# Out projection opened as four side-by-side units without its last two row blocks; norm sums, third gates and first-pass pieces moved later

## Chip, cores, metric

One NeuronCore of one Trainium2 chip runs the whole kernel in one launch. The metric is device time in microseconds (us) of that core, median over runs.

## What is computed

One layer of a hybrid decoder over 2048 prompt tokens with 16 meta tokens ahead of them, and over 8 running sequences of 4 tokens (2096 columns in all, 1024 model dimensions, fp32). A normalised input goes through one input projection. One half of its output feeds an RG-LRU group (causal convolution over 4 taps, two gates, a linear scan), the other half an HGRN2 group (4 heads of 128, gated linear attention with a matrix state). Both outputs, joined, go through one output projection; a squared-ReLU MLP follows.

```python
u = (hn @ w_in)                                  # xa, ga, qb, fb, ib, gb
xc = conv_b + sum(xpad[:, j:j+T] * cw[j] for j in range(4))
r, ig = sigmoid(xh @ w_ra + b_ra), sigmoid(xh @ w_rx + b_rx)
y_a = scan(a, bt) * gelu(ga)
o = rms(hgrn2(silu(q), k, v, logf)) * gn * silu(g)
x = x + concat([y_a, o]) @ w_out
x = x + square(relu(rmsnorm(x) @ w_up)) @ w_down
y = rmsnorm(x)
```

## The kernel before

The columns are worked in two passes (`p` = 0 and 1): 1024 columns in two tiles of 512, then 1072 in three tiles of 358, 358 and 356. Each weight matrix is cut into blocks of 128 output rows, 96 blocks in all: 20 for the four head iterations (V, gate G, XA, F, Q of each), 4 for the GELU gates (GA), 8 for the output projection, 64 for the MLP. A **unit** is one block by one tile: 8 row blocks (the 128-deep slices of the contraction), each with three matmuls, since every fp32 value is split in a rounded high part and a low rest (`hi*hi`, `hi*lo`, `lo*hi`, L411 to L413). A **half unit** is 4 row blocks, 12 matmuls. Units rotate through 4 PSUM banks (`bank`), everything else through 4 more (`aux`). A unit opens when the unit four before it has been read out of its bank.

`schedule(p)` is a table written out by hand: after which half unit (a **slot**, numbered from 0 within an iteration) a **piece** of the attention or gate work is issued. Iteration `i` computes the projections of head `i` and, between them, the pieces of head `i-1`; iteration 4 has the four GA blocks and head 3's pieces. The pieces: VT (transpose v), D (diagonal scores), L1 to L7 (the levels of the decay products, each needing what DVE made of the one before), KT, U (state updates), O (outputs), SS (sum of squares), S1, S2 (reciprocals) and S3 (norm and gate products, DVE alone). GATE is the RG-LRU gates' matmuls, RS, N2 and NF are the ones-matmuls of the three norms, FN and FY the final norm of pass 0, done inside pass 1. `SLOTS` gives the slots, `GATE_SLOT` that of GATE, `FINAL_SLOTS` those of NF, FN and FY.

All engines walk the same table. PE issues (L393 on), DVE reads units out of the banks and does the level products, the state recurrence (`s_in`, eight steps, L1028, semaphore `s_step`; O waits for step `s7`), the convolution (`convolve`, right behind the read-out of the last XA tile, L1137 to L1145), the gate chain and the scan (L1058 to L1076), the reciprocals (L1048) and S3 (L1052, L1054). ACT does sigmoids, square roots, copies and the rounding of activations (`a_hi`), all at the helper's line L601. DVE and ACT run strictly in the order written. In pass 0 the weights come by DMA (SP), ACT rounds them (`round_weights`), DVE or, from the output projection on, POOL makes the low part (L368); in pass 1 POOL's queue reloads the kept parts (L380, L381).

Behind the table, ACT rounds the mixed activations `xy` into `a_hi`, DVE subtracts to `a_lo` (L1233), and PE runs the 8 blocks of the output projection in the order `OUT_ORDER` of row blocks, of which the last, 3, is head 3's. `xy` is then reloaded with the residual by ACT's queue. DVE adds each unit to it (L1243), ACT writes `b_hi` and a square, DVE writes `b_lo` (L1245) and adds up the squares (L1251). The sums over partitions (N2) go to PE once all squares are added; then the MLP starts.

## Time and profile before

| | us |
|---|---|
| median of three runs | 2595.76 |
| the three runs | 2594.53 to 2601.26 |
| profiled execution, its own time | 2603.55 |
| span of that execution, first to last instruction | 2601.9 |
| PE busy in the span | 2493.0 (96%) |
| DVE busy | 1038.5 (40%) |
| ACT busy | 593.5 (23%) |
| POOL busy | 284.1 (11%) |
| granted TensorE clock, mean share of full speed | 0.982 |

The profiled execution took 7.8 more than the median, and its time is 1.65 more than its span. All moments named below are in us from the start of the span. In a row of the timeline the bracket gives the idle time of that engine just before the instruction and what ended it; "x16" is the number of instructions merged in the row. One fp32 matmul of the kernel's `aux` pieces shows as two instructions.

### The profile page before, as it was taken

How to read it: one execution, taken by the hardware profiler on the slowest of the kernel's cores; microseconds unless marked ns; L12 is line 12 of the kernel's file. 1: busy time of each engine (PE TensorE's matmuls, PEld its weight loads, DVE VectorE, ACT ScalarE, POOL GpSimd, SP SyncE). 2: the span in 40 equal slices, each digit the busy share in tenths (PEclk: the TensorE clock that was granted, in tenths of full speed). 3: DMA queues.
4: the chain of work that ended last, by engine and by line, in shares of the span. 5: the costliest groups of instructions: out<-in, count | busy, mean ns of one | idle time of the engine just before them, and what ended most of it. 6: DMA issues, size and time to landing. Idle time of an engine off the chain costs nothing.

```text
span 2601.9 us, 33392 instructions
## 1 busy us (share of the span) xinstructions
PE 2493.0 (96%) x13358; PEld 2235.6 (86%) x13358; DVE 1038.5 (40%) x1603; ACT 593.5 (23%) x961; POOL 284.1 (11%) x275
## 2 busy tenths in 40 slices
PE   5999998999999999999899999999999999999996
PEld 4778877878888888888898988989999999999995
DVE  6676776332121121123756576654321211211224
ACT  4233233332031121223223032132210200200211
POOL 0000001212222122222000000000000000000000
PEclk9999999999999999999999999999999999999998
DMA  5222224434434444353412122133222232222223
GB/s 192 97 98 80 91 97 144 140 133 146 137 141 145 145 139 147 126 204 144 151 61 69 50 65 65 50 142 98 81 81 97 81 97 82 95 85 92 89 89 104
DMA packets 86620, 284.32 MB, mean 109 GB/s; under 512 B 14096, under 2 KB 17296, under 8 KB 86544
## 3 DMA queue, kind: packets, MB, share of 16 engines
q1 hardware_dynamic: 41472, 151.01, 16.9%
q0 software_dynamic: 27648, 100.68, 11.8%
q10 hardware_dynamic: 17424, 31.57, 3.4%
q8 instruction: 53, 0.87, 0.1%
q14 instruction: 23, 0.19, 0.0%
HBM read 171.54 MB, written 111.68 MB: 109 GB/s over the span
## 4 chain that ended last, share of the span: by engine, by line
PE 88%; DVE 9%; ACT 1%; issue 1%; ACTq 1%; DVEq 0%
PE bank L411 26%; PE bank L413 26%; PE bank L412 26%; PE aux L470 4%; DVE ea L1048 1%; DVE attn L979 1%; PE aux L536 1%; PE aux L424 1%; PE aux L460 1%; DVE k L951 1%; DVE a_lo L1187 1%; PE aux L494 1%; DVE q L950 1%; PE aux L513 1%; PE aux L512 1%
## 5 line engine op out<-in xcount | busy, mean ns | idle before, releaser
L411 PE MATMUL bank<-a_hi,w_hi 128*128 128x358 f32 (+2 forms) x2560 | 929.7, 363 | 45.1 <-DVE a_lo L1187 20.6
L413 PE MATMUL bank<-a_hi,w_lo 128*128 128x358 f32 (+2 forms) x2560 | 911.6, 356 | 0.0
L412 PE MATMUL bank<-a_lo,w_hi 128*128 128x358 f32 (+2 forms) x2560 | 910.9, 356 | 0.0
L411 PEld LDWEIGHTS bank<-a_hi,w_hi 128*128 128x128 f32 x2560 | 488.6, 191 | 96.5 <-issue 35.1
L412 PEld LDWEIGHTS bank<-a_lo,w_hi 128*128 128x128 f32 x2560 | 489.2, 191 | 46.9 <-issue 2.9
L413 PEld LDWEIGHTS bank<-a_hi,w_lo 128*128 128x128 f32 x2560 | 488.6, 191 | 45.8
L411 PE MATMUL bank<-b_hi,w_hi 128*128 128x512 f32 (+2 forms) x1280 | 452.9, 354 | 0.0
L413 PE MATMUL bank<-b_hi,w_lo 128*128 128x512 f32 (+2 forms) x1280 | 452.4, 353 | 0.0
L412 PE MATMUL bank<-b_lo,w_hi 128*128 128x512 f32 (+2 forms) x1280 | 452.1, 353 | 0.0
L1274 DVE TENSOR_TENSOR xy<-xy,bank 128x356 f32 (+3 forms) x160 | 94.6, 591 | 564.5 <-PE bank L413 564.5
L368 POOL TENSOR_TENSOR w_lo<-w_st,w_hi 128x1024 fp32r<-128x1024 f32 x74 | 180.9, 2445 | 1045.8 <-ACT w_hi L601 1045.8
L601 ACT ACTIVATE a_hi<-tmp 128x356 f32 (+3 forms) x160 | 88.7, 555 | 833.7 <-DVE tmp L1263 833.7
L411 PEld LDWEIGHTS bank<-b_hi,w_hi 128*128 128x128 f32 x1280 | 240.8, 188 | 23.8 <-issue 0.8
L412 PEld LDWEIGHTS bank<-b_lo,w_hi 128*128 128x128 f32 x1280 | 240.9, 188 | 23.7 <-issue 0.5
L413 PEld LDWEIGHTS bank<-b_hi,w_lo 128*128 128x128 f32 x1280 | 240.6, 188 | 22.0
L1263 DVE SCALAR_TENSOR_TENSOR tmp<-bank,rs 128x356 f32<-128x356 f32 (+1 forms) x160 | 95.1, 594 | 350.4 <-PE bank L413 349.4
L380 POOL DMA_DIRECT2D w_hi<-kept_hi x96 | 50.8, 530 | 1218.9 <-PE bank L413 1218.9
L1266 DVE TENSOR_TENSOR a_lo<-tmp,a_hi 128x356 f32 (+3 forms) x160 | 95.3, 595 | 197.4 <-ACT tmp L601 197.4
L601 ACT ACTIVATE w_hi<-w_st 128x1024 fp32r<-128x1024 f32 x96 | 100.8, 1051 | 277.4 <-PE bank L413 271.9
L470 PEld LDWEIGHTS aux<-q,k 128*128 128x128 f32 x896 | 106.5, 192 | 20.7 <-DVE f L953 18.9
L470 PE MATMUL aux<-q,k 128*128 128x64 f32 x896 | 108.9, 274 | 10.6 <-DVE f L953 10.1
L979 DVE COPY_PREDICATED attn<-mask,aux 128x512 f32<-128x512 int32 (+2 forms) x72 | 50.8, 739 | 96.5 <-PE aux L470 96.5
(150 smaller groups left out, 1557.3 us busy)
## 6 DMA issues: line engine op xcount, KB each, us to landing
w_st<-in_wall SPq DMA_DIRECT2D x96, 512.0 KB, 4.1
kept_hi<-w_hi SPq DMA_DIRECT2D x96, 512.0 KB, 4.8
kept_lo<-w_lo SPq DMA_DIRECT2D x96, 512.0 KB, 5.6
w_hi<-kept_hi POOLq DMA_DIRECT2D x96, 512.0 KB, 3.9
w_lo<-kept_lo POOLq DMA_DIRECT2D x96, 512.0 KB, 4.7
xs<-in_xT ACTq DMA_DIRECT2D x8, 536.0 KB, 6.9
xy<-in_xT ACTq DMA_DIRECT2D x8, 536.0 KB, 6.9
xs<-in_xT ACTq DMA_DIRECT2D x16, 256.0 KB, 6.3
```

What stands on the lines that cost most here:

```text
L368: pool.tensor_tensor(w_lo[:, slot, :], w_st[:, slot, :], w_hi[:, slot, :].bitcast(F32), ALU.subtract).then_inc(w_ready, 1)
L380: pool.dma_start(w_hi[:, slot, :], kept_hi[m]).then_inc(w_again[slot], 16)
L411: pe.matmul(ps, wh, xh, start=(j == 0), stop=False)
L412: pe.matmul(ps, wh, xl, start=False, stop=False)
L413: mm = pe.matmul(ps, wl, xh, start=False, stop=(j == 7))
L424: pe.matmul(open_bank(a)[:, 0:n], ones[:, :], src[:, c0:c0 + n], start=True, stop=True).then_inc(aux_done, 1)
L470: mm = pe.matmul(ps[:, 64 * c:64 * c + 64], k[:, CH * c:CH * c + CH], qv[:, c, :, 1, :], start=True, stop=True)
L601: return nc.scalar.activation(out, in_, func, **kw)
L979: dve.copy_predicated(dst, mk.broadcast_to([r_, nc_, w // x, x]), src).then_inc(aux_free[u % 4], 1)
L1263: stt(z, bank[lu % 4][:, 0:w], 0.0, rs[:, c0:c0 + w], ALU.max, ALU.mult).then_inc(bank_free[lu % 4], 1)
L1266: tt(a_lo[:, 4 * qd + j, c0:c0 + w], z, a_hi[:, 4 * qd + j, c0:c0 + w].bitcast(F32), ALU.subtract).then_inc(h_ready, 1)
L1274: tt(x, x, bank[lu % 4][:, 0:w], ALU.add).then_inc(bank_free[lu % 4], 1)
```

## The change

- `SLOTS[0]`: in pass 0 VT stays at slot 0 and every piece behind it moves one slot later; `GATE_SLOT[0]` goes from 16 to 17. In iteration 4, S1, S2 and S3 leave the table and stand behind it.
- `GATE2`: in pass 1 the gates of the third tile are issued one half unit after the first two (only PE has this piece).
- `FINAL_SLOTS`: NF, FN and FY of pass 0 move from slots 3, 4, 5, 8 to 15 of pass 1 to 8, 9, 10, 12 to 19.
- Output projection: the first four units run row blocks 0, 1, 2, 4, 5, 6 (`EARLY` = 6) one after another, then the last two (7 and 3) of each; the rest run in natural order. ACT and DVE prepare the six blocks of all tiles but the last one during the last GA unit, then the last tile's six, then (DVE) the reciprocals and products of head 3, then the last two blocks of all tiles.
- N2: the first MLP unit is issued ahead of the wait for the squares and the norm sums, with a wait on each `b_lo` tile. For this the first two groups of the MLP's loop are written out.

```diff
+SPLIT_UNITS = 4
+EARLY = 6
...
+def y_no(p, t, n):
+
+    base = KB * NT[0] * p
+    return base + (EARLY * t + n if n < EARLY else EARLY * NT[p] + (KB - EARLY) * t + n - EARLY) + 1
...
-SLOTS = [dict(zip(range(16), PIECES)),
+SLOTS = [dict(zip([0] + list(range(2, 17)), PIECES)),
          dict(zip([0, 4, 5, 6, 8, 9, 10, 12, 13, 14, 15, 16, 18, 19, 21, 22], PIECES))]
-GATE_SLOT = [16, 24]
+GATE_SLOT = [17, 24]
...
-FINAL_SLOTS = {3: ("NF", 0), 4: ("FN", 0), 5: ("FN", 1), **{8 + b: ("FY", b) for b in range(8)}}
+FINAL_SLOTS = {8: ("NF", 0), 9: ("FN", 0), 10: ("FN", 1), **{12 + b: ("FY", b) for b in range(8)}}
...
-                    if i >= 1 and s in SLOTS[p]:
+                    if i >= 1 and s in SLOTS[p] and not (i == HEADS and SLOTS[p][s] in ("S1", "S2", "S3")):
                         pieces.append((SLOTS[p][s], i - 1))
                     if i < HEADS and s == GATE_SLOT[p]:
                         pieces.append(("GATE", i))
+                    if p and i < HEADS and s == GATE_SLOT[p] + 1:
+                        pieces.append(("GATE2", i))
...
+                    for t in ([2] if name == "GATE2" else [0, 1]):
+                        c0, w = TILES[p][t]
...
+                units = [(m, t) for m in range(KB) for t in range(nt)]
+                for m, t in units[:SPLIT_UNITS]:
+                    if t == 0:
+                        weights(p, OUT0 + m)
+                    open_unit(unit_no(p, OUT0 + m, t))
+                    out_unit(m, t, list(range(EARLY)))
+                for m, t in units[:SPLIT_UNITS]:
+                    out_unit(m, t, list(range(EARLY, KB)))
+                for m, t in units[SPLIT_UNITS:]:
+                    if t == 0:
+                        weights(p, OUT0 + m)
+                    open_unit(unit_no(p, OUT0 + m, t))
+                    out_unit(m, t, natural)
...
+                            if first and lu == 0:
+                                pe.wait_ge(b_sum, (KB - 1) * sum(NT[:p + 1]))
+                                for t2, (c2, w2) in enumerate(TILES[p]):
+                                    ones_sum(AUX[(p, "N2", 0)] + t2, rs, c2, w2)
...
+                    if half and blk == OUT0 - 1 and t == NT[p] - 1:
+                        for t2 in range(NT[p] - 1):
+                            round_mix(t2, range(EARLY))
...
+                if p == 0:
+                    round_weights(OUT0 + 1)
+                round_mix(NT[p] - 1, range(EARLY))
...
+                reload_x(range(EARLY))
+                for t in range(NT[p]):
+                    round_mix(t, range(EARLY, KB))
+                reload_x(range(EARLY, KB))
...
+                mix_rest(nt - 1, range(EARLY))
+                for name in ("S1", "S2", "S3"):
+                    piece(p, name, HEADS - 1)
+                for t in range(nt):
+                    mix_rest(t, range(EARLY, KB))
```

Three places in the order of instructions matter below. The first is DVE in iteration 1 of pass 0, around the read-out of the second XA tile (`xpad<-bank`), the convolution (`xc`) and the state recurrence (`s_in`, `state`). Before:

```order
L1105 TENSOR_TENSOR xpad<-bank,rs 128x512
L1118 TENSOR_TENSOR gate<-gate,tmp 128x512
L1016 COPY s_in<-state 128x128
L1028 SCALAR_TENSOR_TENSOR s_in<-s_in,f,aux 128x128 x7
L1028 SCALAR_TENSOR_TENSOR state<-s_in,f,aux 128x128
L1105 TENSOR_TENSOR xpad<-bank,rs 128x512
L1137 COPY xpad<-xhist 128x3
L1143 TENSOR_SCALAR xc<-xpad,par 128x1024
L1145 SCALAR_TENSOR_TENSOR xc<-xpad,par,xc 128x1024 x3
```

After (the same lines of code have other numbers):

```order
L1154 TENSOR_TENSOR xpad<-bank,rs 128x512
L1186 COPY xpad<-xhist 128x3
L1192 TENSOR_SCALAR xc<-xpad,par 128x1024
L1194 SCALAR_TENSOR_TENSOR xc<-xpad,par,xc 128x1024 x3
L1065 COPY s_in<-state 128x128
L1077 SCALAR_TENSOR_TENSOR s_in<-s_in,f,aux 128x128 x7
L1077 SCALAR_TENSOR_TENSOR state<-s_in,f,aux 128x128
```

Before, U stands in slot 10, and its recurrence comes ahead of the second XA tile; after, U stands in slot 11, whose half unit completes that tile, so the read-out and the whole convolution come first.

The second is ACT in the same iteration, from the last F sigmoids to the gates' sigmoids (`ta`, `k_tok`); `tmp<-q` is the sigmoid of the first Q tile. Before:

```order
L601 ACTIVATE k<-f 128x512
L601 ACTIVATE f<-f 128x512
L601 ACTIVATE w_hi<-w_st 128x1024
L601 ACTIVATE ta<-aux,par 128x512
L601 ACTIVATE k_tok<-aux,par 128x512
L601 ACTIVATE ta<-aux,par 128x512
L601 ACTIVATE k_tok<-aux,par 128x512
L601 ACT_TABLE_LOAD
```

After:

```order
L638 ACTIVATE k<-f 128x512
L638 ACTIVATE f<-f 128x512
L638 ACTIVATE w_hi<-w_st 128x1024
L638 ACTIVATE tmp<-q 128x512
L638 ACTIVATE ta<-aux,par 128x512
L638 ACTIVATE k_tok<-aux,par 128x512
L638 ACTIVATE ta<-aux,par 128x512
L638 ACTIVATE k_tok<-aux,par 128x512
L638 ACT_TABLE_LOAD
```

The sigmoid of the first Q tile, which needs DVE to have read that tile out, now stands ahead of the gates' sigmoids. DVE in turn reads that tile behind S3 (`xy<-xy,par,ea`, `xy<-xy,gate`) and ahead of the gate chain:

```order
L1097 RECIPROCAL ea<-ea 128x512
L1263 TENSOR_TENSOR w_lo<-w_st,w_hi 128x1024
L1101 SCALAR_TENSOR_TENSOR xy<-xy,par,ea 128x1024
L1103 TENSOR_TENSOR xy<-xy,gate 128x1024
L1154 TENSOR_TENSOR q<-bank,rs 128x512
L1174 TENSOR_SCALAR f<-f,lbv 128x512
L1175 TENSOR_SCALAR k<-k,lbv 128x512
L1177 TENSOR_SCALAR f<-f 128x512
```

The third is ACT behind the table in pass 0, from the last GELU to the third weight rounding. Before:

```order
L601 ACTIVATE xc<-xc 128x512 x2
L601 ACTIVATE w_hi<-w_st 128x1024
L601 ACTIVATE a_hi<-xy 128x512 x16
L623 DMA xy<-in_xT 128x1024 x8
L601 ACTIVATE b_hi<-xy,par 128x512
L601 ACTIVATE rs<-xy 128x512
L601 ACTIVATE b_hi<-xy,par 128x512
L601 ACTIVATE rs<-xy 128x512
L601 ACTIVATE w_hi<-w_st 128x1024
```

After:

```order
L638 ACTIVATE xc<-xc 128x512
L638 ACTIVATE w_hi<-w_st 128x1024
L638 ACTIVATE a_hi<-xy 128x512 x6
L660 DMA xy<-in_xT 128x1024 x6
L638 ACTIVATE a_hi<-xy 128x512 x4
L660 DMA xy<-in_xT 128x1024 x2
L638 ACTIVATE b_hi<-xy,par 128x512
L638 ACTIVATE rs<-xy 128x512
L638 ACTIVATE b_hi<-xy,par 128x512
L638 ACTIVATE rs<-xy 128x512
L638 ACTIVATE w_hi<-w_st 128x1024
```

The rounding of the mixed activations is now in three parts, and the third weight rounding (block 26) still follows two read-outs of output units.

## Rows read from the trace of the kernel before

**Rows 1.** The page, part 1: busy time, share of the span, instructions
```profile
PE 2493.0 (96%) x13358; PEld 2235.6 (86%) x13358; DVE 1038.5 (40%) x1603; ACT 593.5 (23%) x961; POOL 284.1 (11%) x275
```

**Rows 2.** Stretches: us, then PE, PEld, DVE, ACT, POOL busy (instructions), clock, DMA
```profile
432.90:438.50 5.60, 5.60 (x13) 4.42 (x14) 5.60 (x10) 4.07 (x8) 0.00 (x0) 0.50 0.67 252
585.00:650.00 65.00, 65.00 (x282) 52.66 (x281) 13.12 (x19) 14.00 (x20) 14.40 (x6) 1.00 0.43 146
1885.00:1950.00 65.00, 65.00 (x399) 65.00 (x399) 13.23 (x25) 7.27 (x17) 5.27 (x10) 1.00 0.24 81
```

**Rows 3.** Waits of PE: who for whom, us in total, times, longest us
```profile
PE bank L411 <- DVE a_lo L1233: 15.8, 2, 9.5
PE aux L460 <- DVE q L1120: 8.1, 4, 2.0
PE aux L536 <- ACT ta L601: 6.4, 3, 2.2
PE aux L424 <- DVE rs L1251: 6.1, 2, 3.4
PE aux L424 <- ACT rs L601: 5.6, 1, 5.6
```

**Rows 4.** Timeline of PE in the first pass: start us, us, instruction, idle before
```profile
99.96 2.95 PE L460 MATMUL aux<-q,k 128*128 128x128 f32 x16 [2.03 <-DVE q L1120]
...
187.37 2.02 PE L460 MATMUL aux<-q,k 128*128 128x128 f32 x16 [2.01 <-DVE q L1120]
...
229.10 1.95 PE L494 MATMUL aux<-v_tok,k_tok 128*128 128x128 f32 x16
...
233.66 0.38 PE L512 MATMUL aux<-q,s_in 128*128 128x128 f32 x2
...
240.00 1.88 PE L424 MATMUL aux<-q,ones 128*128 128x512 f32 x4
```

**Rows 5.** Timeline of DVE, the same iteration: state steps, convolution
```profile
230.19 3.07 DVE L1028 SCALAR_TENSOR_TENSOR s_in<-s_in,f,aux 128x128 f32<-128x128 f32 x7 [3.13 <-PE aux L494]
...
233.86 0.69 DVE L1105 TENSOR_TENSOR xpad<-bank,rs 128x512 f32<-128x512 f32 x1 [0.15 <-PE bank L413]
...
235.70 3.92 DVE L1145 SCALAR_TENSOR_TENSOR xc<-xpad,par,xc 128x1024 f32<-128x1024 f32 x3
```

**Rows 6.** Timelines of DVE (two stretches) and ACT around the gates
```profile
183.41 0.69 DVE L1105 TENSOR_TENSOR q<-bank,rs 128x512 f32<-128x512 f32 x1
...
185.20 0.68 DVE L1105 TENSOR_TENSOR q<-bank,rs 128x512 f32<-128x512 f32 x1
...
245.29 6.56 DVE L1048 RECIPROCAL ea<-ea 128x512 f32<-128x512 f32 x2
...
254.80 1.23 DVE L1054 TENSOR_TENSOR xy<-xy,gate 128x1024 f32<-128x1024 f32 x1
255.94 1.22 DVE L1206 TENSOR_TENSOR w_lo<-w_st,w_hi 128x1024 fp32r<-128x1024 f32 x1
...
254.43 0.67 ACT L601 ACTIVATE ta<-aux,par 128x512 f32<-128x512 f32 x1
```

**Rows 7.** Timelines of PE, DVE and POOL at the first out projection
```profile
432.89 0.77 PE L411 MATMUL bank<-a_hi,w_hi 128*128 128x512 f32 x1 [9.49 <-DVE a_lo L1233]
...
428.88 3.26 DVE L1054 TENSOR_TENSOR xy<-xy,gate 128x1024 f32<-128x1024 f32 x1
...
427.95 3.11 POOL L368 TENSOR_TENSOR w_lo<-w_st,w_hi 128x1024 fp32r<-128x1024 f32 x1 [11.87 <-ACT w_hi L601]
...
449.94 2.40 POOL L368 TENSOR_TENSOR w_lo<-w_st,w_hi 128x1024 fp32r<-128x1024 f32 x1 [18.88 <-ACT w_hi L601]
```

**Rows 8.** Timeline of PE at the norm sums of the first pass
```profile
528.00 3.42 PE L424 MATMUL aux<-rs,ones 128*128 128x512 f32 x4 [3.44 <-DVE rs L1251]
```

**Rows 9.** Timeline of DVE at the start of the second pass
```profile
1270.24 0.97 DVE L1105 TENSOR_TENSOR v<-bank,rs 128x358 f32<-128x358 f32 x2
```

**Rows 10.** Timeline of DVE after the second iteration's gates, second pass
```profile
1427.63 0.53 DVE L1105 TENSOR_TENSOR q<-bank,rs 128x358 f32<-128x358 f32 x1
```

More of the change, by code:

```diff
@@ L154, in aux_uses @@
 def aux_uses(p, name):
-    if name in ("FN", "FY", "S1", "S2", "S3"):
+    if name in ("FN", "FY", "S1", "S2", "S3", "GATE2"):
         return 0
@@ L400, in weights, with products @@
                     pe.wait_ge(w_ready, blk + 1)
-            def half_unit(u, slot, hi, lo, c0, n, korder, half, ready=None, first=0):
+            def products(u, slot, hi, lo, c0, n, korder, js, ready=None, count=None):
                 ps = bank[u % 4][:, 0:n]
-                for j in range(4 * half, 4 * half + 4):
+                for j in js:
                     if ready is not None:
-                        pe.wait_ge(ready, first + j)
+                        pe.wait_ge(ready, count(j))
                     kb = korder[j]
@@ L413, in half_unit, with halves @@
                     mm = pe.matmul(ps, wl, xh, start=False, stop=(j == 7))
-                if half:
+                if js[-1] == KB - 1:
                     mm.then_inc(unit_done, 1)
+            def halves(half):
+                return list(range(4 * half, 4 * half + 4))
             def open_bank(a):
@@ L530, in piece @@
                         ones_sum(a + s, q, lo_, hi_ - lo_)
-                elif name == "GATE":
-                    pe.wait_ge(rg_step, rg_at(p, i, "sc3" if p else "c3"))
-                    for t, (c0, w) in enumerate(TILES[p]):
+                elif name in ("GATE", "GATE2"):
+                    if name == "GATE":
+                        pe.wait_ge(rg_step, rg_at(p, i, "sc3" if p else "c3"))
+                    a = AUX[(p, "GATE", i)]
+                    for t in ([2] if name == "GATE2" else [0, 1]):
+                        c0, w = TILES[p][t]
                         for g, wt in enumerate((w_ra, w_rx)):
@@ L569, in _, with out_unit @@
-                pe.wait_ge(b_sum, (KB - 1) * sum(NT[:p + 1]))
-                for t, (c0, w) in enumerate(TILES[p]):
-                    ones_sum(AUX[(p, "N2", 0)] + t, rs, c0, w)
-                pe.wait_ge(b_lo_ready, KB * (nt + (NT[0] if p else 0)))
-                hb = p * 8 * NT[0] * FF_GROUPS
-                with pe.Fori(0, FF_GROUPS) as g:
+                def out_unit(m, t, js):
+                    products(unit_no(p, OUT0 + m, t), (OUT0 + m) % 2, a_hi, a_lo, *TILES[p][t], OUT_ORDER, js,
+                             y_ready if m == 0 else None, lambda j: y_no(p, t, j))
@@ new lines, in _, with quad @@
+                hb = p * 8 * NT[0] * FF_GROUPS
+                def quad(g, stage, qd, first=False):
+                    for j in range(4):
+                        blk = MLP0 + 8 * stage + j
+                        if p:
+                            pe.wait_ge(w_again[j % 2], 256 * g + 64 * qd + 32 * (blk // 2 + 1))
+                        else:
+                            pe.wait_ge(w_ready, 16 * g + 4 * qd + (blk + 1))
+                        for t, (c0, w) in enumerate(TILES[p]):
+                            lu = j * nt + t
+                            pe.wait_ge(bank_free[lu % 4], 4 * nt * g + nt * qd
+                                       + (unit_no(p, MLP0 + 8 * stage, 0) // 4 + lu // 4))
+                            if stage and j == 0:
+                                pe.wait_ge(h_ready, 8 * nt * g + (hb + 7 * nt + t + 1))
+                            hi, lo = (a_hi, a_lo) if stage else (b_hi, b_lo)
+                            for half in range(2):
+                                products(lu, j % 2, hi, lo, c0, w, natural, halves(half),
+                                         b_lo_ready if first and j == 0 else None,
+                                         lambda kb: KB * NT[0] * p + kb * nt + t + 1)
+                            if first and lu == 0:
+                                pe.wait_ge(b_sum, (KB - 1) * sum(NT[:p + 1]))
+                                for t2, (c2, w2) in enumerate(TILES[p]):
+                                    ones_sum(AUX[(p, "N2", 0)] + t2, rs, c2, w2)
@@ L576, in _ @@
+                quad(0, 0, 0, first=True)
+                quad(0, 0, 1)
+                with pe.Fori(0, 2) as qd:
+                    quad(0, 1, qd)
+                with pe.Fori(1, FF_GROUPS) as g:
                     for stage in range(2):
                         with pe.Fori(0, 2) as qd:
[L578 to L594 removed]
@@ L790, in _, with round_mix @@
                     load_state(0)
+                def round_mix(t, ns):
+                    c0, w = TILES[p][t]
+                    act.wait_ge(unit_done, unit_no(p, OUT0 - 1, t) + 1)
+                    for n in ns:
+                        b = OUT_ORDER[n]
+                        if b < HEADS:
+                            act.wait_ge(o_inv, O_STEPS * (4 * p + b) + O_STEPS)
+                        else:
+                            act.wait_ge(post, post_no(p, 3, b - HEADS, NT[p] - 1) + 1)
+                        fn(a_hi[:, b, c0:c0 + w], xy[:, b, c0:c0 + w], ACT.Copy).then_inc(y_hi, 1)
                 queue = []
@@ L1211, in _ @@
                         started = True
+                    if half and blk == OUT0 - 1 and t == nt - 1:
+                        for t2 in range(nt - 1):
+                            mix_rest(t2, range(EARLY))
                     if half:
```

62 lines of the change are left out of this document (16 added, 46 removed).

## The prediction

> **What bounds the kernel now.** The page's busy times come first: PE is busy for 2493.0 of the span's 2601.9 [rows 1], so no other engine is the bound, and what can be won is the time in which PE stands or runs slowly. The stretches give PE's pace: 282 matmuls of 512 columns in 65 us (0.231 each) and 399 of 358 or 356 columns (0.163 each) [rows 2]. So a half unit, 12 matmuls, takes 2.77 in the first pass and 1.96 in the second. The first of those stretches also shows the other level of the clock: behind a long stand PE starts only 13 matmuls in 5.6 us at a granted clock of 0.50, which is 1.2 GHz; at full clock it would have started 24, so some 2.6 are lost. The waits of PE then name where it stands [rows 3]: twice for the mixed activations ahead of the out projection (15.8), four times for the query at piece D (8.1), three times for an aux bank at the gates' third tile (6.4), twice for the squares ahead of the norm sums (6.1), once for ACT's square root at the start of the second pass (5.6). That is 42.0, and the change is aimed at all of it. The question is what is late next at each place.
>
> **First pass, piece O.** U now follows slot 11, which completes the second XA tile, and DVE works strictly in its written order: tile read-out, convolution, and only then the state recurrence. Before, O followed U's start by 233.66 - 229.10 = 4.56 [rows 4] without a wait. Read-out and convolution take from 233.86 to 235.70 + 3.92 = 239.62, that is 5.76, beginning 0.2 behind the half unit; the seven state steps that O waits for take from 230.19 on, 3.07 [rows 5]. With 0.2 for the copy of the state and 0.2 for the signal, O can start 0.2 + 5.76 + 0.2 + 3.07 + 0.2 = 9.4 after U's start, so PE waits 9.4 - 4.56 = 4.9. Iterations 1 to 3 have a convolution: **+14.7**. Iteration 4 has two GELU operations of about 0.65 in its place: **+0.4**.
>
> **First pass, piece D.** D and GATE both move by one slot, and from the sums SS to D there are as many half units and pieces as before, so PE reaches D just as long after SS. What changes is the query. Before, ACT's first gate sigmoid came at 254.43, 14.4 after the sums at 240.00 [rows 4, 6]. Now the first Q tile's sigmoid stands ahead of it, and DVE reads that tile only behind both reciprocals (6.56), S3 and the weight split, which ended at 255.94 + 1.22 = 257.16, 17.2 after the sums [rows 6]. The first reciprocal can start about 0.9 sooner, with the F read-out behind it, giving 16.3; with 0.7 for the read-out and 0.6 for its sigmoid the gates' sigmoids start at 17.6, 3.2 later than before. In return the chain behind the scan is shorter by the first Q read-out and F's finishing, 185.20 - 183.41 = 1.8 [rows 6]. The wait of 2.0 becomes 2.0 + 3.2 - 1.8 = 3.4 in iterations 2 to 4. Iteration 1 follows an iteration with no head behind it, DVE is free for the tile, and the wait falls to 2.0 - 1.8 = 0.2. In all 10.4 where 8.1 stood: **+2.4**. The short waits between the levels L1 to L3 stay, as both their sides keep their distance.
>
> **The clock in the first pass.** The trace does not show gaps of 3.4 and 4.9 here. Nearest are: a gap of 2.03 with D's sixteen matmuls taking 2.95, and one of 2.01 with 2.02 for the same work [rows 4], so that a gap may cost nothing; and the 2.6 lost behind a gap of 9.49 [rows 2, 7]. I take 2.2 behind each of three waits of 4.9 and 1.2 behind each of three of 3.4, together 10.2, less the 3.5 that the present D gaps cost in the first and last iteration (0.9 in D and about as much behind it): **+6.7**, with 0 - 3.5 and 6 x 2.6 - 3.5 = 12.1 as the ends. By the Trainium skill, TensorE: Matmul & The Clock Gate, section HAM oscillation, stands of this kind send the clock to its lower level each time; by it the term would be its upper end.
>
> **First out projection.** Counted from the end of the last GA half unit, PE before stood 9.49, ran four units of 24 matmuls (22.1) and lost 2.6 [rows 2, 7]: 34.2 to block 26. After, four units with six row blocks give 16.6 of work. DVE ends the six last-tile subtractions at 7.7, the reciprocals 6.6 later and the products 2.5 later, at 16.8, and the last four subtractions at 19.3; PE ends the four units at 23.1, nearly without a stand. But block 26 may be rounded only when block 24's units are done, and its rounding stands on ACT behind two read-outs of output units. Before they were early, and POOL's split behind it, at 449.94, took 2.40 [rows 7]. Now they come in a burst: DVE reads at 19.3 and, after ACT's two operations and `b_lo`, at 22.6; ACT rounds at 24.6 to 25.7, POOL splits until 28.2. PE stands from 23.1 to 28.3 and loses 2 at low clock behind it. The rounding of block 25 adds a split beside DVE's subtractions. Before, a split and DVE's product of two SBUF operands ran side by side, 3.11 and 3.26, where alone they take 2.40 and 1.23 [rows 6, 7]: I add 2.0. GPSIMD Engine Reference, Specifications, in the Trainium skill has the two engines share their SBUF interfaces when DVE has two SBUF inputs; by this rule, the trace agrees. Were there no sharing, the term would be 2.0 better. 28.3 + 2 + 2 = 32.3: **-1.9** (0 to -6, where no clock is lost and no split disturbs).
>
> **Norm sums.** The first MLP unit (5.5, and 3.9 in the second pass) covers the waits of 3.4 and 2.7 [rows 3, 8]; the four sums took 3.42 where four of the same size take 1.88 at full clock [rows 4, 8]. Two waits, 6.1, twice 1.5 and about 0.2 behind each: **-9.5**. What is late next is DVE's reciprocal of the norm (6.6), with three more free banks, 16.6 of PE work, to cover it.
>
> **Start of the second pass.** NF no longer waits 5.6 for ACT. But unit 4 opens in the bank of the first V tile, which DVE reads only at 1270.24, behind the reciprocals of RS [rows 9]. PE came to NF's wait, which ended at 1262.4, at 1256.8, one sum behind slot 3, so without NF it ends slots 4 to 7 7.8 after 1255.7, at 1263.5, and stands until 1270.8; with 2.4 of low clock and 1.7 for NF behind slot 8 it is at 1274.9, where it now is at about 1262.4 + 1.1 + 7.8 + 2.5 = 1273.8: **+1.1** (ends -2 and +3).
>
> **Third gates.** The half unit hides the 2.1 [rows 3]. But the second V tile (slot 2 of the next iteration) opens in the bank of the first Q tile, which DVE reads behind the gate chain, at 1427.63 to 1428.1 [rows 10]; PE reached it at about 1428.7 (an estimate: a gate wait that ended at 1411.2, two sums, seven half units of 1.96, VT and 2 of low clock). So only some 0.6 of slack, and 0.6 more where ACT's last sigmoid comes sooner, is kept: -2.5 over three iterations. In iteration 0 ACT waited for nothing, the chain shifts by the half unit: +1.9. The stand moved to slot 2 costs clock that slack had hidden, 1 each: **+3** (-4 to +7).
>
> **Second out projection.** PE's four early units last 11.8, while DVE needs about 17.7 for subtractions, reciprocals and products; the last two row blocks start 6 later. The wait of 15.8 - 9.5 = 6.3 [rows 3] comes back inside: **-0.7** (-3 to +2).
>
> Sum: 14.7 + 0.4 + 2.4 + 6.7 - 1.9 - 9.5 + 1.1 + 3 - 0.7 = +16.2. The profiled execution's own 2603.55 becomes 2619.8. It stood 7.8 above the median of 2595.76; the median becomes **2612.0**.
>
> **Rivals.**
> Faster: piece O does not wait. What decides is whether DVE is through with convolution and seven steps within 4.56 of U's start; by the rows it needs 9.4, so it would have to run in another order than written. For it: before, it was in time. Then 14.7 and its 6.6 of clock fall away: 2595.8 - 5.1 = 2590.7. Chance 0.12.
> Same: all waits come, but with no clock lost behind them (as at 187.37) and no split beside the subtractions. 10.2 in the first pass, 2 + 2 at the out projection and 1 at the gates fall away: 16.2 - 15.2 = +1.0, 2596.8; with half of it 2604. Chance 0.16.
> Slower still: each new stand pays the whole 2.6: 12.1 for 6.7, and 3 more in the second pass: 2620.4. The 9.49 gap speaks for it, 187.37 against it. Chance 0.12. That is what the section of the Trainium skill's TensorE page named above would give.
> The change does not do what it says in the second pass, where six row blocks are too little work: that is within the forecast.
>
> **How the numbers follow.** The forecast has 0.60. A measurement of this kernel can tell about 0.3%, 7.8, from no change. Slower than 2603.6: nearly all of the forecast, the costlier clock and a little of the second rival, 0.72; within 2588.0 to 2603.6: 0.16; faster: 0.12. The range runs from 2597 (the second rival) to 2624 (the clock at its upper end, with the gates' end).
>
> **What would show it.** Right: in the waits of PE, O (the matmul on `s_in`) for DVE's state steps, three times near 4.9, and D for the query near 0.2 once and 3.4 three times; the wait for N2 and the 9.5 gone; a wait of about 5 for the split of block 26; near 7 for a V read-out at the start of the second pass; about 6 inside its out projection. PEclk lower in the first pass. Wrong: no wait at O, or D waits gone in all iterations.

## The result and the profile after

| | before | after |
|---|---|---|
| median, us (five runs each, interleaved) | 2595.76 | 2611.21 |
| lowest to highest | 2594.53 to 2601.69 | 2609.63 to 2615.19 |
| profiled execution, its own time | 2603.55 | 2615.19 |
| its span | 2601.9 | 2613.5 |
| granted clock, mean | 0.982 | 0.980 |

The ratio is 1.0054, with a 95% interval from 1.0042 to 1.0065: the change makes the kernel slower by 15.45. Forecast were 2612.0, a range of 2597 to 2624, and 0.72 for slower. The two profiled executions differ by less, 11.6, as the one before stood 7.8 above its median and the one after 4.0; so what is read from their rows is good to a few us.

A stand is time in which PE has nothing that it may start. The waits of PE in the kernel after the change (who for whom, us in total, times, longest us), to be read against [rows 3]:

```profile
PE bank L423 <- DVE a_lo L1236: 21.1, 3, 17.2
PE aux L528 <- DVE s_in L1077: 14.4, 4, 4.7
PE bank L423 <- DVE v L1154: 14.2, 2, 8.7
...
PE aux L476 <- DVE q L1169: 8.7, 4, 2.8
PE bank L423 <- DVE q L1154: 7.8, 4, 2.0
PE bank L423 <- DVE a_lo L1252: 7.7, 2, 5.5
PE bank L423 <- POOL w_lo L380: 4.0, 1, 4.0
```

What the change was aimed at is gone: no wait for the squares `rs`, none for ACT's square root, no aux bank held by `ta`, and the wait ahead of the out projection has fallen from 15.8 to 7.7. In its place stand four groups that were not there: piece O for the state (14.4), a bank held by a Q tile (7.8), 5.6 more for a V tile (14.2 where 8.7 stood), and POOL's weight split (4.0). D's wait for the query stayed. The first row is the wait at the kernel's start, which the change does not touch.

Where O and D stand, in the timeline of PE of the same kernel (start us, us, instruction, idle before), first pass:

```profile
154.63 0.79 PE L528 MATMUL aux<-q,s_in 128*128 128x128 f32 x2 [4.73 <-DVE s_in L1077]
...
197.03 3.75 PE L476 MATMUL aux<-q,k 128*128 128x128 f32 x16 [2.81 <-DVE q L1169]
...
251.08 0.80 PE L528 MATMUL aux<-q,s_in 128*128 128x128 f32 x2 [4.72 <-DVE s_in L1077]
...
293.06 2.02 PE L476 MATMUL aux<-q,k 128*128 128x128 f32 x16 [2.81 <-DVE q L1169]
...
387.37 3.63 PE L476 MATMUL aux<-q,k 128*128 128x128 f32 x16 [2.81 <-DVE q L1169]
```

And DVE ahead of the O at 251.08:

```profile
241.82 0.69 DVE L1154 TENSOR_TENSOR xpad<-bank,rs 128x512 f32<-128x512 f32 x1 [4.32 <-PE bank L425]
...
243.68 3.93 DVE L1194 SCALAR_TENSOR_TENSOR xc<-xpad,par,xc 128x1024 f32<-128x1024 f32 x3
247.64 0.23 DVE L1065 COPY s_in<-state 128x128 f32<-128x128 f32 x1
247.97 3.05 DVE L1077 SCALAR_TENSOR_TENSOR s_in<-s_in,f,aux 128x128 f32<-128x128 f32 x7
```

DVE is idle for 4.32 until the XA tile is complete, then works without a pause: read-out, convolution, copy, seven state steps. U had started at 241.62, so O comes 9.46 behind it; the forecast had 9.4.

To see the clock, the stretches from one D to the next (us, PE busy (instructions), granted clock, DMA share, GB/s). They hold the same work. Before:

```profile
99.96:187.37 87.41, 84.52 (x444) 0.98 0.26 91
187.37:273.17 85.80, 82.89 (x445) 1.00 0.27 92
```

After:

```profile
103.45:197.03 93.58, 85.15 (x445) 0.96 0.25 85
197.03:293.06 96.03, 87.60 (x444) 0.95 0.24 83
293.06:387.37 94.31, 85.90 (x445) 0.96 0.25 84
```

PE's *busy* time grew too, by 0.6 in the first of these stretches and 4.7 in the second, for the same instructions, where the mean clock fell to 0.95 and 0.96. That part of the loss stands in no list of waits.

The first out projection, in the timelines of PE, DVE, POOL and ACT of the kernel after (the last GA half unit ends at 449.4):

```profile
455.95 0.77 PE L423 MATMUL bank<-a_hi,w_hi 128*128 128x512 f32 x1 [2.23 <-DVE a_lo L1252]
...
479.72 0.80 PE L423 MATMUL bank<-a_hi,w_hi 128*128 128x512 f32 x1 [4.03 <-POOL w_lo L380]
...
446.88 3.71 DVE L1252 TENSOR_TENSOR a_lo<-xy,a_hi 128x512 fp32r<-128x512 f32 x6 [3.20 <-ACT a_hi L638]
...
453.36 2.44 DVE L1252 TENSOR_TENSOR a_lo<-xy,a_hi 128x512 fp32r<-128x512 f32 x1 [0.77 <-ACT a_hi L638]
...
452.88 2.37 POOL L380 TENSOR_TENSOR w_lo<-w_st,w_hi 128x1024 fp32r<-128x1024 f32 x1 [17.12 <-ACT w_hi L638]
...
477.32 2.34 POOL L380 TENSOR_TENSOR w_lo<-w_st,w_hi 128x1024 fp32r<-128x1024 f32 x1 [22.07 <-ACT w_hi L638]
...
475.68 0.61 ACT L638 ACTIVATE rs<-xy 128x512 f32<-128x512 f32 x1
476.20 1.04 ACT L638 ACTIVATE w_hi<-w_st 128x1024 fp32r<-128x1024 f32 x1
```

The first early unit ends at 453.6 and the second, which reads the last tile, stands 2.23: the first subtraction of that tile, begun while POOL's split ran, took 2.44, where six alone took 3.71. The last two row blocks come without any wait. Block 26's weights are late by 4.03, as its rounding (476.20) stands on ACT behind two read-outs.

In the second pass, timelines of PE and DVE of the kernel after:

```profile
1289.15 0.67 PE L423 MATMUL bank<-a_hi,w_hi 128*128 128x358 f32 x1 [5.56 <-DVE v L1154]
...
1345.97 0.43 PE L423 MATMUL bank<-a_hi,w_hi 128*128 128x358 f32 x1 [1.86 <-DVE q L1154]
...
1745.64 0.67 PE L423 MATMUL bank<-a_hi,w_hi 128*128 128x358 f32 x1 [5.45 <-DVE a_lo L1252]
...
1281.66 6.88 DVE L970 RECIPROCAL rs<-rs 128x358 f32<-128x358 f32 x3 [4.70 <-DMA spad<-in_conv]
1288.57 1.40 DVE L1154 TENSOR_TENSOR v<-bank,rs 128x358 f32<-128x358 f32 x3
```

The norm sums behind the first MLP unit, in PE's timeline, now come without a stand and at full clock:

```profile
553.49 1.88 PE L440 MATMUL aux<-rs,ones 128*128 128x512 f32 x4
```

The two waits removed at the start of the second pass and at its gates are each followed by one on the next thing that was late: the V tile that DVE reads only behind its reciprocals (5.56 where ACT's square root cost 5.6), and a Q tile's bank (1.86 to 2.04, four times) where the gates had waited 2.1 three times.

### The profile page after: what moved, and what is told of

Read it like the earlier page. It is cut to its first block, busy times and chain, and to the rows that moved or that the text cites. A ratio compares the mean times of both kernels' runs of the same rounds, so it can differ in the third digit from the quotient of the medians.

```text
span 2613.5 us, 33374 instructions
## 1 busy us (share of the span) xinstructions
PE 2497.5 (96%) x13358; PEld 2241.2 (86%) x13358; DVE 1039.8 (40%) x1603; ACT 596.2 (23%) x963; POOL 283.4 (11%) x275
## 3 DMA queue, kind: packets, MB, share of 16 engines
q0 software_dynamic: 27648, 100.68, 11.8%
## 4 chain that ended last, share of the span: by engine, by line
PE 73%; DVE 8%; issue 3%; ACT 1%; POOL 0%; DMA 0%; ACTq 0%; DVEq 0%; POOLq 0%
PE bank L423 23%; PE bank L425 23%; PE bank L424 22%; PE aux L486 2%; DVE ea L1097 1%; DVE attn L1028 1%; DVE k L1000 1%; DVE xc L1194 1%; DVE q L999 1%; DVE xy L1123 0%; DVE a_lo L1236 0%; DVE xy L980 0%; PE aux L476 0%; ACT ta L638 0%; PE aux L510 0%
## 5 line engine op out<-in xcount | busy, mean ns | idle before, releaser
L638 ACT ACTIVATE tmp<-tmp 128x356 f32<-128x356 f32 (+1 forms) x160 | 86.1, 538 | 0.0
```

What stands on the lines that cost most here:

```text
L638: return nc.scalar.activation(out, in_, func, **kw)
```

## The experiments

Each variant has 4 to 11 timed executions, beside 15 or 21 of the kernel before. The median of the latter was 2596.03, 2596.04 and 2596.38 in the three groups of four (runs 1 to 4; 5 to 8; 9 to 12), so that times of different groups can be compared. The first group asks whether the first pass's pieces carry the loss, and which wait carries which part.

**1. Pieces back.**

```diff
-SLOTS = [dict(zip([0] + list(range(2, 17)), PIECES)),
+SLOTS = [dict(zip(range(16), PIECES)),
-GATE_SLOT = [17, 24]
+GATE_SLOT = [16, 24]
```

> The changed kernel with the first-pass pieces back in slots 0 to 15 and the first gates in slot 16; the split out projection, the late norm sums and the third gates stay. Theory (the moved pieces cost the first pass some 24 us): the four O waits of 4.7, 4.7, 4.7 and 0.2 go, the four D waits come back at 2.0 each (8.1 in all, as before the change) in place of 8.7, and the clock loss behind the O and D waits (some 7 to 9 us over the pass) goes; the first pass ends 22 to 25 us earlier, and the kernel takes 2586 to 2590 us, 6 to 9 below the kernel before. Rival (the out projection's split and the norm sums, not the pieces, are what costs): the time stays above 2600 us.

Measured: 2585.62 (2582.34 to 2587.37), ratio to before 0.9961, interval 0.9947 to 0.9975. That is 25.6 below the changed kernel, 0.4 beyond the better end of the expected range. O does not wait, D waits four times, 8.1 in all. The theory holds: the table of slots costs 25.6, and all the rest of the change together gains 10.4 over the kernel before.

**2. Convolution behind the pieces (first pass).**

```diff
                         if un[1] == 5 * un[0] + XA and un[0] < HEADS and un[2] == nt - 1:
-                            convolve(p, un[0])
+                            if p:
+                                convolve(p, un[0])
+                            else:
+                                conv_due = un[0]
...
                     for name, i in pieces:
                         if name not in ("RS", "NF", "GATE2"):
                             piece(p, name, i)
+                    if conv_due is not None:
+                        convolve(p, conv_due)
+                        conv_due = None
```

> The changed kernel, with VectorE's convolution of the first pass issued behind the pieces of its slot instead of ahead of them, so that the recurrence U, its read-outs and s_in come first. Theory (O waits because the convolution stands ahead of U on VectorE): the O waits of 4.7 go, the D waits stay at 2.8, 14.4 us of waiting and up to 3 us of clock loss come back, some 2594 to 2598 us. Rival (the s_in chain is bound by something else, or the convolution, now later, makes the D or q step later by as much): less than 5 us come back, over 2606 us.

Measured: 2590.55 (2585.11 to 2594.9), ratio 0.9978 (0.9969 to 0.9988): 20.7 below the changed kernel, more than expected. DVE and PE in the timeline of this variant:

```profile
233.23 0.69 DVE L1154 TENSOR_TENSOR xpad<-bank,rs 128x512 f32<-128x512 f32 x1 [4.33 <-PE bank L425]
233.83 0.22 DVE L1065 COPY s_in<-state 128x128 f32<-128x128 f32 x1
234.16 3.06 DVE L1077 SCALAR_TENSOR_TENSOR s_in<-s_in,f,aux 128x128 f32<-128x128 f32 x7
...
238.64 3.92 DVE L1194 SCALAR_TENSOR_TENSOR xc<-xpad,par,xc 128x1024 f32<-128x1024 f32 x3
...
237.59 0.38 PE L528 MATMUL aux<-q,s_in 128*128 128x128 f32 x2
```

The same operations, with the state steps ahead of the convolution; O starts 4.56 behind U's 233.03, as before the change [rows 4], and without a stand. D still waits 2.8. So the O wait is VectorE's order and nothing else. Of the 20.7, the vanished waits are 14.2; the other 6.5 I put down to the clock (the executions of this variant lie up to 9.8 apart, so this share is rough). The forecast had priced the clock behind the three O waits at 2.2 each, 6.6; my expectation for this run, up to 3, was the poorer number.

**3. The first gates in slot 16, the pieces still moved.**

```diff
-GATE_SLOT = [17, 24]
+GATE_SLOT = [16, 24]
```

> The changed kernel with only the first pass's gates back in slot 16, the pieces still moved. Theory (D of the next head waits for q because the gates' steps on the other engines come one slot later): the D waits of 2.8 go or fall under 0.5, the O waits stay at 4.7; 8 us of waiting and up to 3 us of clock loss come back, some 2599 to 2604 us. Rival (D's wait hangs on the pieces alone): D still waits 2.0 or more, and the time stays at 2609 to 2612 us.

Measured: 2596.56 (2594.41 to 2601.17), ratio 1.0006 (0.9997 to 1.0015), 14.65 below the changed kernel: beyond the expected range on the good side. The wait for `q` has left the list of waits altogether, O's four waits stand at 14.4. Waits of 8.7 and some 6 of clock came back. So D hangs on how far the gates stand ahead of it, not on where D is.

**4. Both edits.**

> Both edits: the convolution behind the pieces of its slot and the first gates in slot 16, with the pieces still one slot later than before. Theory (the two waits are independent): neither O nor D waits over 0.5 us, some 23 to 27 us come back, 2584 to 2588 us, the fastest of the four. Rival (one wait is what holds the other back): the sum of the two gains is not reached, and this is at 2590 us or above.

Measured: 2578.03 (2571.96 to 2579.61), ratio 0.9926 (0.9913 to 0.994): 33.2 below the changed kernel and 18 below the kernel before. Expected had been 23 to 27; again clock is what was priced too low. The gains of runs 2 and 3 add up to 35.4, within what the medians scatter; the two waits are independent. The stretches from D to D of this variant, with the columns as above:

```profile
102.23:185.82 83.59, 82.70 (x445) 1.00 0.28 95
185.82:269.45 83.63, 82.72 (x446) 1.00 0.29 95
```

This is what an iteration takes without a stand: 83.6, at full clock. It is the yardstick for the others. The changed kernel's 93.58, 96.03 and 94.31 hold 7.5 of waits each (4.7 and 2.8), so 2.5, 4.9 and 3.2 are clock; the kernel before has 2.0 of waits in each, and 1.8, 0.2 and 0.2 of clock.

**5. The slots alone, on the kernel before.** The same two lines of run 1 the other way round, and S1 to S3 of the last head behind the table:

```diff
-                    if i >= 1 and s in SLOTS[p]:
+                    if i >= 1 and s in SLOTS[p] and not (i == HEADS and SLOTS[p][s] in ("S1", "S2", "S3")):
...
+                for name in ("S1", "S2", "S3"):
+                    piece(p, name, HEADS - 1)
```

> The kernel before the change, with one part of the change alone: the first-pass pieces one slot later, the first gates in slot 17, and the last head's weight split S1 to S3 behind the table. Theory (the moved pieces cost the first pass what the changed kernel lost there): O waits 4.7 three times, D 2.8 three times, with their clock loss, about 24 us, and the wait ahead of the out projection grows by a half unit, 2.8, as the last head's sums SS come so much nearer to its end: 2619 to 2625 us. Rival (the loss comes only together with the split out projection or the late norm sums): under 2612 us.

Measured: 2627.99 (2627.52 to 2628.49), ratio 1.0116 (1.01 to 1.0131), 32 above the kernel before and 3 beyond the expected range. The waits of this variant:

```profile
PE bank L411 <- DVE a_lo L1236: 23.8, 2, 12.0
...
PE aux L512 <- DVE s_in L1028: 14.4, 4, 4.7
...
PE aux L460 <- DVE q L1120: 8.7, 4, 2.8
```

O and D wait exactly as in the changed kernel, with none of its other parts there. What I had missed is the second pass: S1 to S3 leave its table too, so DVE comes to its reciprocals later, and the wait ahead of the out projection grows in both passes, by 2.5 and by 5.5 (12.0 and 11.8 where 9.5 and 6.3 stood [rows 3]). The 24 that were expected for O, D and their clock, and these 8.0, give the 32; with the 25.6 of run 1 they would give 33.6, so the split into parts is good to a us or two. The full change, with its split out projection, has waits of 2.2 and 5.5 in these two places.

**6. Block 26's weights rounded earlier, on top of run 4.**

```diff
-                    if m and p == 0:
+                    if m > 1 and p == 0:
                         round_weights(OUT0 + m + 1)
                     for t, (c0, w) in enumerate(TILES[p]):
...
+                        if p == 0 and m == 0 and t == 1:
+                            round_weights(OUT0 + 2)
```

> The variant with the convolution behind the pieces and the first gates in slot 16, and in addition the first pass rounds block 26's weights ahead of the second output unit's read-out on ScalarE. Theory (the wait of 4.0 for POOL's split of block 26 is ScalarE's order, read-outs ahead of the rounding): the wait falls to 1 to 2, with less clock loss behind it; 2.5 to 5 us come back, some 2573 to 2576 us. Rival (the rounding cannot start earlier, since it also needs block 24's units done, or the read-outs that it passes free banks that are needed): no gain, 2577 us or more.

Measured: 2573.38 (2570.94 to 2573.96), ratio 0.9906 (0.9891 to 0.9921), 4.65 below run 4, as expected; but the intervals of the two ratios touch (run 4 has 0.9913 to 0.994), so the times alone leave the size open. ACT, POOL and PE of this variant:

```profile
435.85 0.61 ACT L638 ACTIVATE rs<-xy 128x512 f32<-128x512 f32 x1
436.37 1.04 ACT L638 ACTIVATE w_hi<-w_st 128x1024 fp32r<-128x1024 f32 x1
437.88 0.72 ACT L638 ACTIVATE b_hi<-xy,par 128x512 fp32r<-128x512 f32 x1 [0.47 <-DVE xy L1312]
...
437.50 2.37 POOL L380 TENSOR_TENSOR w_lo<-w_st,w_hi 128x1024 fp32r<-128x1024 f32 x1 [19.50 <-ACT w_hi L638]
...
439.92 0.50 PE L423 MATMUL bank<-a_hi,w_hi 128*128 128x512 f32 x1 [1.41 <-POOL w_lo L380]
```

The rounding now stands between the first and the second read-out (the two `b_hi`), and the wait is 1.41 where it was 4.04. Behind the wait of run 4 the granted clock stood at 0.50 for 3.4 us; behind this one it stayed at 1.00.

**7. Third gates back beside the first two, on top of run 4.**

```diff
-                    if p and i < HEADS and s == GATE_SLOT[p] + 1:
-                        pieces.append(("GATE2", i))
...
-                    for t in ([2] if name == "GATE2" else [0, 1]):
+                    for t in range(NT[p]):
```

> The variant with the convolution behind the pieces and the first gates in slot 16, with the second pass's third gates back beside the first two. Theory (the third gates' move gained about 1.3: the aux waits of 2.1 went, the slot 2 bank waits of 1.9 to 2.0 came, but clock that stood low before the change did not drop): the ta wait comes back three times at 2.1, the slot 2 waits go, 0 to 2.5 us slower than that variant, 2578 to 2581 us. Rival (my forecast: the move costs 3): 2 to 4 us faster, 2574 to 2576 us.

Measured: 2575.63 (2574.04 to 2576.47), ratio 0.9912 (0.9896 to 0.9927), 2.4 below run 4. The wait for `ta` is back, 5.8 over three times, and the bank wait for a Q tile (7.9 in run 4) is gone from the list. The forecast's sign is the better one, my later reading of the two profiles (a gain of 1.3) was not; but the intervals of runs 4 and 7 overlap, and in run 9 against run 6 the same edit brings only 0.7. It gains nothing to move these gates; that it costs 3 isn't settled.

**8. PE's order in the out projections plain again, on top of run 4.**

```diff
-SPLIT_UNITS = 4
+SPLIT_UNITS = 1
```

> The variant with the convolution behind the pieces and the first gates in slot 16, with TensorE's order in the out projections as plain units again (each unit all eight row blocks; VectorE and ScalarE keep the order six, then two). Theory (the split covers the wait for the last two row blocks): the first unit stands 11 to 12 in the first pass and some 14 in the second, the wait for block 26's split goes; 8 to 9 us worse in each pass, 2591 to 2598 us. Rival (most of that time comes back later, as the banks' read-outs and block 26's weights were the bound of the split order): under 2586 us.

Measured: 2594.86 (2590.28 to 2595.9), ratio 0.9986 (0.9977 to 0.9995), 16.8 above run 4, as expected. PE in this variant:

```profile
432.08 0.79 PE L423 MATMUL bank<-a_hi,w_hi 128*128 128x512 f32 x1 [14.80 <-DVE a_lo L1252]
...
1717.18 0.67 PE L423 MATMUL bank<-a_hi,w_hi 128*128 128x358 f32 x1 [14.26 <-DVE a_lo L1252]
```

Without the three other early units, the first unit stands 14.8 and 14.3 for the last two row blocks. In run 4 these places read 2.24 (for the first subtraction of the last tile) and 5.46.

**9. Runs 6 and 7 together, 10. and NF, FN, FY in their old slots as well.** Run 10 adds, to run 9:

```diff
-FINAL_SLOTS = {8: ("NF", 0), 9: ("FN", 0), 10: ("FN", 1), **{12 + b: ("FY", b) for b in range(8)}}
+FINAL_SLOTS = {3: ("NF", 0), 4: ("FN", 0), 5: ("FN", 1), **{8 + b: ("FY", b) for b in range(8)}}
```

> Four edits on the changed kernel: the convolution behind the pieces, the first gates in slot 16, block 26 rounded ahead of the second output unit's read-out, the third gates beside the first two. Theory (the last two gains, 4.7 and 2.4, are independent, as they lie in different passes): 7 below the variant with the first two edits, some 2571 us. Rival (a gain in the first pass is given back where the second starts): 2573 us or more.

> The same four edits, and the first pass's final norm and outputs back in slots 3 to 5 and 8 to 15 of the second pass. Theory (moving NF gained nothing, since a V tile's read-out waits instead): NF waits about 4 to 5.6 for ScalarE's square root, the bank wait of 5.6 for the V tile goes, the time is within 2 of the variant with four edits. Rival (my forecast: the move costs 1.1): 1 faster, which these rounds can hardly tell.

Measured: run 9 2572.73 (2567.82 to 2574.49), ratio 0.99 (0.9884 to 0.9915); run 10 2572.02 (2571.18 to 2576.35), ratio 0.9908 (0.9893 to 0.9923). Run 9 is 5.3 below run 4, not the whole 7. It is as fast as anything tried: 23.7 below the kernel before, 38 below the changed one. Run 10 is the same within 1: NF waits 4.49 for ACT's square root there, and the V tile's 7.15 of run 9 is gone. Moving NF exchanges one wait for the other.

**11. Pieces in their old slots, the first gates one slot earlier still.** The early rounding of block 26 and the third gates beside the first two stay from run 9, the convolution's edit goes, and:

```diff
-SLOTS = [dict(zip([0] + list(range(2, 17)), PIECES)),
+SLOTS = [dict(zip(range(16), PIECES)),
-GATE_SLOT = [17, 24]
+GATE_SLOT = [15, 24]
```

> The changed kernel with the first-pass pieces back in slots 0 to 15 and the first gates one slot ahead of where they were before the change, in slot 15; block 26 rounded early and the third gates beside the first two. Theory (what D waits for is how many slots lie between the last head's gates and D, not where the pieces stand): D waits nowhere, O neither, the wait ahead of the last row blocks in the first pass is 1.4 in place of 2.2, some 2569 to 2573 us. Rival (the gates, in the slot of S3 and nearer to SS, wait themselves or hold up the weight split): D or the gates wait 1 to 2 each iteration, 2576 us or more.

Measured: 2600.39 (2595.32 to 2601.13), ratio 1.0008 (0.9999 to 1.0017). My theory said 2569 to 2573. The rival (2576 or more) was right in the time and in naming the weight split, though not in the size of the waits. ACT, DVE and PE of this variant:

```profile
259.53 0.68 ACT L636 ACTIVATE ta<-aux,par 128x512 f32<-128x512 f32 x1
...
269.70 1.04 ACT L636 ACTIVATE w_hi<-w_st 128x1024 fp32r<-128x1024 f32 x1
...
271.25 2.35 DVE L1123 TENSOR_TENSOR_SCAN xy<-ta,hprev,k_tok 128x1024 f32<-128x1024 f32 x1
...
274.03 1.23 DVE L1263 TENSOR_TENSOR w_lo<-w_st,w_hi 128x1024 fp32r<-128x1024 f32 x1
...
275.31 0.80 PE L421 MATMUL bank<-a_hi,w_hi 128*128 128x512 f32 x1 [4.53 <-DVE w_lo L1263]
```

D and O wait for nothing, as the theory had it. But the gates now stand ahead of a block's weight rounding on ACT, and the whole gate chain, scan included, runs before `w_hi` and `w_lo`: PE stands 3.06 once and 4.54 three times for its weights, 16.7 in all, and its clock falls behind each. In runs 1 and 4 the gates are in slot 16 and the rounding goes ahead of their sigmoids (in run 1 at 254.95 and 255.89). I had counted the slots between gates and D, and not what else stands around slot 15 in ACT's queue.

**12. Norm sums ahead of the first MLP unit again, on the changed kernel.**

```diff
-                            if first and lu == 0:
-                                pe.wait_ge(b_sum, (KB - 1) * sum(NT[:p + 1]))
-                                for t2, (c2, w2) in enumerate(TILES[p]):
-                                    ones_sum(AUX[(p, "N2", 0)] + t2, rs, c2, w2)
...
+                pe.wait_ge(b_sum, (KB - 1) * sum(NT[:p + 1]))
+                for t2, (c2, w2) in enumerate(TILES[p]):
+                    ones_sum(AUX[(p, "N2", 0)] + t2, rs, c2, w2)
                 quad(0, 0, 0, first=True)
```

> The changed kernel with the norm sums ahead of the first MLP unit again, in both passes. Theory (the first MLP unit hides two waits of 2.7 and 3.4 and the clock loss behind them): both come back, with 1.5 of slower sums each, 9 to 10 us slower than the changed kernel, 2619 to 2622 us. Rival (VectorE's reciprocal of the norm, now later, already took back part of it): under 2616 us.

Measured: 2623.42 (2620.67 to 2624.51), ratio 1.0103 (1.0087 to 1.0118), 12.2 above the changed kernel, where 9 to 10 were expected. PE in this variant:

```profile
547.61 2.94 PE L440 MATMUL aux<-rs,ones 128*128 128x512 f32 x4 [3.45 <-DVE rs L1310]
...
1833.96 2.63 PE L440 MATMUL aux<-rs,ones 128*128 128x358 f32 x6 [2.69 <-DVE rs L1310]
```

Both waits are back at their old size, 6.1, with slow sums behind them. But from the end of the out projection to the second MLP unit this variant's profiled execution takes only 3.6 (first pass) and 2.8 (second) more than the changed kernel's, 6.4 in all. The rest of the 12.2 is not located; much of it may be the scatter of two medians, whose intervals allow for 8 as well.

## Why the prediction was right

Term by term, with what the profile or a run gave:

| term | forecast | measured | from |
|---|---|---|---|
| O waits, first pass | +14.7 and +0.4 | +14.2 and +0.2 | waits; run 2 |
| D waits | +2.4 | +0.6 (8.7 for 8.1) | waits; run 3 |
| clock, first pass | +6.7 | some +8.6 | stretches; runs 2 to 4 |
| the three together | +24.2 | +25.6 | run 1 |
| first out projection | -1.9 | some -2.7 | stretches |
| norm sums | -9.5 | -12.2, or -7.9 | run 12, or stretches |
| NF, start of second pass | +1.1 | 0 within 1 | run 10 |
| third gates | +3 | +0.7 to +2.4 | runs 7 and 9 |
| second out projection | -0.7 | some -1.4 | stretches |
| all parts but the slots | -8.0 | -10.4 | run 1 |
| sum | +16.2 | +15.45 | |

(The clock's 8.6: from the first D to the last SS the changed kernel takes 442.12 - 103.45 = 338.67 and run 4 406.25 - 102.23 = 304.02, which is 34.65 less; 22.6 of it are waits and 12.0 clock. The kernel before takes 413.2 - 99.96 = 313.24, 9.22 over run 4, with 5.85 of waits and 3.4 of clock. First out projection: from the last GA half unit to its end 528.00 - 3.44 - 423.40 = 101.16 before, 547.90 - 449.40 = 98.50 after. Second: from the sums SS of head 3 to its end 114.85 before, 113.47 after. Norm sums: from there to the start of the second MLP unit 11.8 and 9.1 before, 7.3 and 5.7 after.)

The mechanisms named in the prediction were found, each where it was said to be. That the total comes within 0.8 is luck beyond that: the parts miss by up to 2.7 and cancel, the O and D waits less and the clock more than forecast, and a median scatters by more than 0.8 itself.

**Piece O** was right in mechanism and size: 4.9 forecast, 4.72 measured, and run 2 shows that VectorE's written order alone makes the wait.

**Piece D** was right in mechanism and 0.6 too large each time: 0.2 once and 3.4 three times were forecast, 0.24 and 2.81 came. (10.4 less 8.1 is 2.3, where the prediction writes 2.4.) The gates' sigmoids started 276.39 - 259.08 = 17.3 after the sums, not 17.6; the rest of the excess lies in the chain behind them.

**The clock** behind the new stands had to be taken between 0 and 6 x 2.6 = 15.6, and the rows of gaps of 2.0 and 9.49 did not decide. The value taken, 10.2 in all, proved a little low against the 12.0 of the stretches. The rivals that hung on it fail: the clock did fall (against "same"), and not behind every stand (against "slower still", 2620.4): the D at 293.06 took 2.02 behind the same gap of 2.81 behind which those at 197.03 and 387.37 took 3.75 and 3.63. By the Trainium skill, TensorE: Matmul & The Clock Gate, section HAM oscillation, waits of TensorE of some 3 to 5 us between bursts of matmuls send the clock down each time. This trace agrees for the three O stands of 4.7, behind each of which the granted clock is 0.50. The D stands of 2.81 are shorter than those that the section describes, and behind two of the three the clock is 0.50 as well, behind the third 1.00.

**First out projection.** Counted from the last GA half unit, block 26 was forecast at 28.3 and, with the clock, in effect 32.3. It started at 479.72 - 449.4 = 30.3, and with the 1.5 lost behind it that is 31.8. The parts were less well placed: "nearly without a stand" was wrong by the 2.23 at 455.95, which the clash of POOL and DVE makes, and the wait for block 26 was 4.0 for 5.2. The clash itself, put at +2.0, shows in 2.44 for a subtraction that takes 0.62 alone: 1.8.

**Second out projection and start of the second pass.** The waits were forecast at about 6 and 7 and measured 5.45 and 5.56. The -0.7 is more than the figures beside it give (17.7 - 11.8 = 5.9 for 6.3, -0.4).

**Third gates.** Both waits came as forecast, the one for `ta` gone and one for the bank of a Q tile in its place, 1.86 to 2.04. Its sum does not come out at 3 either: -2.5 and +1.9, with 1 of clock behind each of three or four stands, are +2.4 or +3.4. The runs put it at +0.7 to +2.4.

**The norm sums** gained 12.2 by the medians of run 12 and 7.9 by the stretches of the two profiles, with 9.5 forecast between them. Only with the smaller figure do the parts add up to run 1's -10.4: -2.7 - 7.9 + 0 - 1.4 and +0.7 to +2.4 are -11.3 to -9.6.

The rival "faster" (O does not wait) fell with the 14.4 of the waits. Run 2, which builds that case, gives 2590.55; the rival had worked it out at 2590.7. Its executions run from 2585.11 to 2594.9, so agreement this close is chance too.

## What to carry to other kernels

When a piece is moved by a slot, list for every engine what it now comes behind, and count the time from the producer's last input to the consumer: here 9.4 against 4.6 was to be read off the rows of the kernel before. Both expensive waits, and run 11's loss, come from an in-order queue on an engine that is only 23 to 40% busy; in runs 2, 3 and 6 the repair was to put what TensorE waits for ahead of what it does not, which cost nothing that these runs show. And a removed wait is worth what it saves up to the next late producer: NF's and the third gates' moves exchanged one wait for another of the same size.

## What was not expected

- **A stand of TensorE costs here about half as much again as the list of waits says.** In the first pass of the changed kernel 22.6 of waits (beyond run 4's) went with 12.0 of lower clock. Removing 14.2 of waits gave 20.7, removing 8.7 gave 14.65. Three of my expectations (runs 2 to 4) priced this too low; the forecast, at 10.2, came nearer.
- **The same gap does not always cost the same.** Behind gaps of 2.81, D's matmuls took 3.75, 2.02 and 3.63 in one execution; in run 12, whose first pass has the same table, 2.02, 3.62 and 3.63. Over the profiled executions of the two kernels and runs 1, 2, 3, 5 and 12, D took longer than the undisturbed 2.02 behind 3 of 8 gaps of 2.0 and 9 of 12 gaps of 2.8, and O's first matmuls ran at low clock behind 12 of 12 gaps of 4.7. What decides between like gaps was not tried. It also moves the time of one and the same kernel: run 4's executions took 2571.96 at a mean clock of 0.988 and 2578.01 to 2579.61 at 0.985. The 7.8 that the profiled execution before stood above its median may be of this kind: from the second MLP unit to the last head's SS it took 1163.2 at a mean clock of 0.98, the same stretch in run 5, with the same table of the second pass, 1156.5 at 0.99.
- **Where POOL and DVE collided here, they did not share a rate: one stood until the other was through.** The subtraction of 453.36 lasted until 455.80, which is 0.55 after POOL's split ended at 452.88 + 2.37 = 455.25, and 0.62 is its time alone. [Rows 7] read the same way: DVE's product ended at 428.88 + 3.26 = 432.14, 1.08 after POOL's 427.95 + 3.11 = 431.06, and alone it takes 1.23; POOL's split, begun 0.9 before DVE's operation ahead of that product ended (427.56 + 1.28 = 428.84), took 0.7 more than the 2.40 it takes alone. The split of 452.88 found DVE's preceding operation, begun at 451.10, done after 1.49 and took 2.37. The forecast had read these rows as a shared rate. By the Trainium skill, SBUF — State Buffer, section SBUF: two separate sides, the two take a port pair as an exclusive lock for a whole instruction, and the later one blocks; this trace agrees.
